# Gated memory of the first mixer: four decay buffers, three broadcast banks, block-wise masks and weights

## The reference

```python
def mlstm_scan(q, k, v, ig, lf, state):
    # h_t = C_t q_t / max(|n_t . q_t|, 1)
    ...
        dmat = jnp.where(tril, bcum[..., :, None] - bcum[..., None, :] + ic[..., None, :], -jnp.inf)
        m_t = jnp.maximum(m_inter, jnp.max(dmat, axis=-1))
        s = jnp.einsum('bhtd,bhsd->bhts', qc, kc) * jnp.exp(dmat - m_t[..., None])
        num = jnp.einsum('bhts,bhse->bhte', s, vc) + w_inter[..., None] * jnp.einsum('bhtd,bhed->bhte', qc, cmat)
        den = jnp.sum(s, axis=-1) + w_inter * jnp.einsum('bhtd,bhd->bht', qc, nvec)
        h = num / jnp.maximum(jnp.abs(den), jnp.exp(-m_t))[..., None]
```

## Time and profile before

| what | us |
|---|---|
| median of 3 runs (2557.1 to 2558.24) | 2557.97 |
| the profiled execution | 2560.64 |
| its span in the profile | 2558.8 |
| TensorE busy in the span | 2370.4 |
| the stage of the change, first row to last `mem_done` (1163.32 to 1234.83) | 71.51 |
| TensorE busy in it | 53.66 |
| VectorE busy in it | 39.92 |
| ScalarE busy in it | 33.42 |

### The profile page before, as it was taken

How to read it: one execution, slowest core, us unless ns; L and a number is a source line. 1 busy time by engine, 2 the same in 40 slices (tenths; PEclk the granted TensorE clock), 3 DMA queues, 4 the chain that set the end, 5 groups by cost and what they waited for, 6 DMA issues and landing times. The chain is left out here.

```text
span 2558.8 us, 36168 instructions
## 1 busy us (share of the span) xinstructions
PE 2370.4 (93%) x13368; PEld 1898.6 (74%) x13368; DVE 1182.8 (46%) x2007; ACT 870.9 (34%) x1369; POOL 160.8 (6%) x140
## 2 busy tenths in 40 slices
PE   4898989999999999987899999999999999987998
PEld 2665778787777777955667777767888877956998
DVE  1423636563443345365553433334343344545665
ACT  1321635552222133245442221224232234235544
POOL 1001120220000010040100000010000010000000
PEclk7998999999999999997999999999999998988999
DMA  7554064236565432300255565552233232303574
GB/s 232 161 165 140 25 174 144 80 108 189 153 213 154 119 99 76 92 16 17 66 154 159 173 189 161 160 164 74 83 110 94 73 108 75 99 1 99 164 207 122
DMA packets 514708, 312.85 MB, mean 122 GB/s; under 512 B 15911, under 2 KB 513166, under 8 KB 514478
## 3 DMA queue, kind: packets, MB, share of 16 engines
q1 hardware_dynamic: 507056, 309.16, 41.2%
q10 hardware_dynamic: 7550, 2.33, 0.4%
HBM read 310.41 MB, written 1.05 MB: 122 GB/s over the span
## 5 line engine op out<-in xcount | busy, mean ns | idle before, releaser
L840 PE MATMUL ps<-h_hi,w_hi 128*128 128x512 f32 (+1 forms) x2208 | 807.1, 366 | 30.9 <-DVE h_lo L1274 13.0
L840 PE MATMUL ps<-h_lo,w_hi 128*128 128x512 f32 (+1 forms) x2208 | 793.4, 359 | 0.0
L840 PE MATMUL ps<-h_hi,w_lo 128*128 128x512 f32 (+1 forms) x2208 | 793.1, 359 | 0.0
L840 PEld LDWEIGHTS ps<-h_hi,w_hi 128*128 128x128 f32 x2208 | 421.5, 191 | 131.5 <-issue 46.3
L1417 DVE TENSOR_TENSOR w_lo<-stage,w_hi 128x1024 fp32r<-128x1024 f32 x244 | 304.8, 1251 | 368.5 <-ACT w_hi L1084 367.9
L840 PEld LDWEIGHTS ps<-h_hi,w_lo 128*128 128x128 f32 x2208 | 421.0, 191 | 68.1
L840 PEld LDWEIGHTS ps<-h_lo,w_hi 128*128 128x128 f32 x2208 | 421.8, 191 | 63.6
L1084 ACT ACTIVATE w_hi<-stage 128x1024 fp32r<-128x1024 f32 x244 | 254.9, 1055 | 476.2 <-PE ps L840 237.9
L1417 DVE TENSOR_TENSOR w_lo<-deep,w_hi 128x1024 fp32r<-128x1024 f32 x184 | 225.2, 1234 | 280.6 <-ACT w_hi L1084 279.2
L840 PE MATMUL ps<-g_hi,w_hi 128*128 128x512 f32 (+1 forms) x704 | 261.0, 371 | 0.3
L840 PE MATMUL ps<-g_lo,w_hi 128*128 128x512 f32 (+1 forms) x704 | 257.6, 366 | 0.0
(11 more groups left out here) (340 smaller groups left out, 2422.7 us busy)
## 6 DMA issues: line engine op xcount, KB each, us to landing
modw<-in_ada_w SPq DMA_DIRECT2D x72, 1024.0 KB
stage<-in_ffn_w_in SPq DMA_DIRECT2D x88, 512.0 KB, 4.6
deep<-in_ffn_w_in SPq DMA_DIRECT2D x88, 512.0 KB, 3.9
modw<-in_w_mod SPq DMA_DIRECT2D x24, 1024.0 KB
stage<-in_w_in SPq DMA_DIRECT2D x44, 512.0 KB, 4.6
stage<-in_ffn_w_out SPq DMA_DIRECT2D x32, 384.0 KB, 3.5
stage<-in_even_w_in SPq DMA_DIRECT2D x24, 512.0 KB, 3.9
deep<-in_ffn_w_out SPq DMA_DIRECT2D x32, 384.0 KB, 3.5
```

What stands on the lines that cost most here:

```text
L840: last = mm(ps[:, j, 0:b - a], w_part[wp][:, u % RING, c, :], x_part[xp][:, x, a:b], start=first and wp == xp, stop=final and wp == "lo")
```

## The change

- Four decay buffers in place of two, of 1280 elements each: two in `big`, one in `vtok`, one in `mixT`. The exponentials of stream j now wait for `numden` of stream j-4.
- Three banks for the broadcast row, 3, 4 and 7, and three `dargs`. `maxima_row(j)` and `args(j)` now wait for `decay` of stream j-3; row 2 waits for the attention's last `att_evac`, which frees bank 7.
- A stream's weights lie by block: `diagonal` (the four blocks of 128x128 in which keys and queries are the same tile), `full` (the one block of tokens and the one of context that is wholly seen) and `across` (context keys for tokens). Only `diagonal` is masked, so `args` is one instruction of 512 elements. The exponentials are eight: four of 128x128 from `dargs`, two of 128x128 and two of 128x256 from the bank.
- `products(h)` is six products of 256 columns in place of two of 512 and two of 256, laid in the banks as the weights are.
- `weighted(j)` is three plain multiplications (512, 256 and 512 elements) in place of four with a factor. The factor 1/8 is left out of numerator and denominator; the floor of the denominator is multiplied by 8 instead.
- Orders: TensorE runs rows 0 to 2 ahead of `products(0)`, and row j+3 in each turn. VectorE runs `weighted(j)`, `memory(j-1)`, `args(j+3)` and then the feed.

```diff
-        decay = big[:, 4 * NT:10 * NT].rearrange("p (s t r q) -> p s t r q", s=2, t=2, r=3)
-        dargs = mixT[:, 0:4, :].rearrange("p (s t) (r q) -> p s t r q", s=2, r=2)
+        decay = [big[:, 4 * NT:4 * NT + 1280], big[:, 7 * NT:7 * NT + 1280], vtok[:, 0:2, :].rearrange("p a d -> p (a d)")[:, 0:1280],
+                 mixT[:, 4:7, :].rearrange("p c n -> p (c n)")[:, 0:1280]]
+        dargs = mixT[:, 0:3, :].rearrange("p s (r a q) -> p s r a q", r=2, a=2)
...
+        ROW_BANK = (3, 4, 7)
@@ TensorE
-                if j >= 2:
-                    eng.wait_ge(S("decay"), p.at("decay", j - 1))
+                if j >= 3:
+                    eng.wait_ge(S("decay"), p.at("decay", j - 2))
+                elif j == 2:
+                    eng.wait_ge(S("att_evac"), p.at("att_evac", N2))
...
                 for a in range(2):
-                    mm(ps[:, a, :], k[:, SEQ + a * P:SEQ + a * P + P], q, start=True, stop=True)
-                    last = mm(ps[:, 2, a * SEQ:a * SEQ + SEQ], k[:, a * P:a * P + P], q[:, 0:SEQ], start=True, stop=True)
+                    near, far = (k[:, at + a * P:at + a * P + P] for at in (0, SEQ))
+                    for bank, keys, at in ((0, near, 0), (1, far, SEQ), (2, far, 0)):
+                        last = mm(ps[:, bank, a * SEQ:a * SEQ + SEQ], keys, q[:, at:at + SEQ], start=True, stop=True)
...
-            maxima_row(0)
+            for j in range(3):
+                maxima_row(j)
             products(0)
-            maxima_row(1)
             for j in range(8):
-                if j + 2 < 8:
-                    maxima_row(j + 2)
+                if j + 3 < 8:
+                    maxima_row(j + 3)
@@ ScalarE
-                if j >= 2:
-                    eng.wait_ge(S("numden"), p.at("numden", j - 1))
-                for a in range(2):
-                    act(decay[:, j % 2, a, 0, :], dargs[:, j % 2, a, 0, :], ACT.Exp, bias=a_of(a))
-                    act(decay[:, j % 2, a, 1, :], ps[:, 3 + j % 2, 0:SEQ], ACT.Exp, bias=a_of(2 + a), scale=-1.0)
-                    last = act(decay[:, j % 2, a, 2, :], dargs[:, j % 2, a, 1, :], ACT.Exp, bias=a_of(2 + a))
+                if j >= 4:
+                    eng.wait_ge(S("numden"), p.at("numden", j - 3))
+                for r in range(2):
+                    for a in range(2):
+                        act(diagonal[:, r, a, :], dargs[:, j % 3, r, a, :], ACT.Exp, bias=a_of(2 * r + a))
+                    act(full[:, r, :], mrow[:, r, 1 - d, :], ACT.Exp, bias=a_of(2 * r + d), scale=-1.0)
+                for s in range(2):
+                    last = act(across[:, s, :], ps[:, ROW_BANK[j % 3], 0:SEQ], ACT.Exp, bias=a_of(2 + s), scale=-1.0)
@@ VectorE
-                if j >= 2:
-                    eng.wait_ge(S("decay"), p.at("decay", j - 1))
...
+                if j >= 3:
+                    eng.wait_ge(S("decay"), p.at("decay", j - 2))
+                up(V.scalar_tensor_tensor(dargs[:, j % 3].rearrange("p r a q -> p (r a) q"), ps[:, ROW_BANK[j % 3], :].rearrange("p (b q) -> p b q", q=P), -1.0,
+                                          mmask[:, j % 2, 0, 0:P].unsqueeze(1).broadcast_to([P, TT, P]), ALU.mult, ALU.add), "args")
...
+                V.tensor_tensor(diagonal, diagonal, qk[:, :, 0::3, :], ALU.mult)
+                V.tensor_tensor(full, full, qk[:, :, 1 + j % 2, :], ALU.mult)
+                up(V.tensor_tensor(across, across, ps[:, 2, :].rearrange("p (s q) -> p s q", s=2), ALU.mult), "weighted")
...
-                link(V.scalar_tensor_tensor(dc, den, -1.0, floor, ALU.mult, ALU.max))
-                link(V.tensor_tensor(dc, den, dc, ALU.max))
+                link(V.scalar_tensor_tensor(dc, floor, HD ** 0.5, den, ALU.mult, ALU.max))
+                link(V.scalar_tensor_tensor(dc, den, -1.0, dc, ALU.mult, ALU.max))
...
             for j in range(8):
                 weighted(j)
+                if j:
+                    memory(j - 1)
+                if j + 3 < 8:
+                    args(j + 3)
                 if j == 2:
                     dve_feed(eng, p, (0, 1))
                 if j == 5:
                     dve_feed(eng, p, (2,))
-                if j + 2 < 8:
-                    args(j + 2)
-                if j:
-                    memory(j - 1)
```

More of the change, by code:

```diff
@@ L1945, in memory @@
                 h, d = j // 2, j % 2
+                diagonal, full, across = decay_parts(j)
                 eng.wait_ge(S("weighted"), p.at("weighted", j + 1))
@@ L1950, in memory @@
                     eng.wait_ge(S("ones_set"), p.at("ones_set", 1))
[L1951 to L1961, removed]
+                for r in range(2):
+                    for a in range(2):
+                        terms = [(diagonal[:, r, a, :], 2 * r + a)]
+                        if a != d:
+                            terms.append((full[:, r, :], 2 * r + d))
+                        if r == 0:
+                            terms += [(across[:, s, a * P:a * P + P], 2 + s) for s in range(2)]
+                        for n, (w, tile) in enumerate(terms):
+                            last = mm(ps[:, 5 + r, a * (P + 1):(a + 1) * (P + 1)], w, vm[:, tile, h, :], start=n == 0, stop=n == len(terms) - 1)
                 up(last, "numden")
-            maxima_row(0)
+            for j in range(3):
+                maxima_row(j)
             products(0)
-            maxima_row(1)
             for j in range(8):
-                if j + 2 < 8:
-                    maxima_row(j + 2)
+                if j + 3 < 8:
+                    maxima_row(j + 3)
                 if j % 2 and j < 7:
@@ L2175, in weighted @@
                 eng.wait_ge(S("qk_done"), p.at("qk_done", j // 2 + 1))
-                for t_ in range(2):
-                    w = decay[:, j % 2, t_]
-                    V.scalar_tensor_tensor(w[:, 1:3, :], ps[:, t_, :].rearrange("p (r q) -> p r q", r=2), HD ** -0.5, w[:, 1:3, :],
-                                           ALU.mult, ALU.mult)
-                    last = V.scalar_tensor_tensor(w[:, 0, :], ps[:, 2, t_ * SEQ:t_ * SEQ + SEQ], HD ** -0.5, w[:, 0, :], ALU.mult, ALU.mult)
-                up(last, "weighted")
+                diagonal, full, across = decay_parts(j)
+                qk = ps[:, 0:2, :].rearrange("p r (b q) -> p r b q", q=P)
+                V.tensor_tensor(diagonal, diagonal, qk[:, :, 0::3, :], ALU.mult)
+                V.tensor_tensor(full, full, qk[:, :, 1 + j % 2, :], ALU.mult)
+                up(V.tensor_tensor(across, across, ps[:, 2, :].rearrange("p (s q) -> p s q", s=2), ALU.mult), "weighted")
             def memory(j):
@@ L2205, in dve_even @@
             eng.wait_ge(S("consts_in"), 16 * (CONST_LOADS + 1))
-            args(0)
-            args(1)
+            for j in range(3):
+                args(j)
             for j in range(8):
                 weighted(j)
+                if j:
+                    memory(j - 1)
+                if j + 3 < 8:
+                    args(j + 3)
                 if j == 2:
```

15 lines of the change are left out of this document (9 added, 6 removed).

## The result

The changed kernel takes 2545.26 us (median of 4 runs, 2539.42 to 2546.94), the kernel before, on the same chip, 2558.1 (4 runs, 2557.1 to 2560.6). The ratio is 0.9944, with a 95% interval of 0.9927 to 0.9962, so it is faster: by 12.8 us between the medians, by 14.3 according to the ratio (9.7 to 18.7 by its interval). The ratio is estimated over all runs of both kernels and need not be the quotient of the medians. The forecast was 2541.7 and a gain of 16.3.

A forecast was written before the change was run, and what follows sets the result against it. TensorE paces the program; its waits and half clock lengthen the 71.5 us stage. A full-clock path of 49.2 plus 3.0 and 3.0 for the clock gives 55.2, gain 16.3: 2557.97 to about 2541.7 us, 8 in 10 within 2535 to 2551.

The forecast's parts named there:

- The start: Stage start on TensorE: rows 1 and 2 fill the gap before products 0, idle 1.6 us in place of 3.05.
- The exponentials: ScalarE, per stream: eight smaller ones taken at 2.45 us, between 1.9 and 3.1; six before took 2.4.
- The products: TensorE: 2.58 us a head at full clock as before, added weight loads at nothing, 2.6 us in all as bound.
- The waits: TensorE ahead of memories: backward 1.9 us each at memories 2, 4 and 6, forward 1.5 at memory 7.
- The feed ahead of `weighted(3)`: VectorE after memory 1: 6.25 us until products 2 may start, against TensorE's 5.2; 1.2 us more with a semaphore.
- The path at full clock: TensorE's stage: memories, products, rows and waits from memory 0 sum to 39.4 us; stage of 49.2 against 71.5.
- The clock: Half clock in the stage: 3.0 us from the fall at the start, 3.0 from one stretch around the feed.
- the step from the profile to the median: Whole program: the gain of 16.3 us taken off the median 2557.97, though the profiled execution lay 2.67 above it.
- the argument that the clock never rose during such work: TensorE's rows and first products: 64-row inputs bring no rise, so the fall at the start should stay.
- full clock throughout: Rival for the stage, chance 0.15: 1.6 us of idleness bring no fall; stage 49.2, gain 22.3, time 2535.7 us.
- The order alone: Rival for the stage, chance 0.15: half-clock busy time stays 34.46 us, costing 17.2; stage 66.4, gain 5.1, time 2552.9.

The follow-up runs named there:

- e1: The changed kernel run and profiled once more, nothing altered: 2542.84 us, ratio 0.9945 to the kernel before, stage 54.61 us.
- e3: The changed kernel with rows 1 and 2 behind the first products on TensorE: 2549.16 us, ratio 0.9963 to the kernel before, stage 58.72 us.
- e8: The kernel before with only row 1 ahead of the first products and VectorE's memory, args, feed order: 2551.94 us, ratio 0.9958, stage 58.27 us.
- e9: The changed kernel with VectorE's two-unit feed one turn later, behind args(6) instead of args(5): 2550.81 us, ratio 0.9963 to the kernel before, stage 58.63 us.
- e5: The changed kernel with six unread filler products of 128 rows ahead of the first products: 2544.92 us, ratio 0.9945 to the kernel before, stage 54.04 us.
- e12: The changed kernel with 128-row fillers wherever TensorE waits and ScalarE's third-unit feed one turn later: 2545.42 us, ratio 0.9942 to the kernel before, stage 51.64 us.
- e2: The changed kernel with two decay buffers in use instead of four: 2544.73 us, ratio 0.9948 to the kernel before, stage 54.79 us.
- e11: The changed kernel with VectorE's args issued once more, unread, for streams 2 to 7: 2546.84 us, ratio 0.9953 to the kernel before, stage 55.88 us.
- e6: The changed kernel with six unread filler products of 64 rows ahead of the first products: 2547.04 us, ratio 0.9940 to the kernel before, stage 55.30 us.
- e7: The kernel before with twelve 128-row fillers each ahead of the first products and memories 2 and 4: 2550.58 us, ratio 0.9958, stage 57.54 us.
- e4: The kernel before with only VectorE's order changed to weighted(j), memory(j-1), args(j+2), then the feed: 2555.49 us, ratio 0.9984, stage 62.26 us.
- e10: The changed kernel with VectorE's feed one turn later and 128-row fillers wherever TensorE waits: 2544.33 us, ratio 0.9938 to the kernel before, stage 54.13 us.

## Why the prediction was right

The size, 16.3 us by the stage, was measured as 16.6; the path with its steps came out nearly term by term. Since the stage of before is the same 71.51 in both, this tests the stage of the changed kernel: 55.2 forecast, 54.93 and 54.61 measured.

- **The start.** Memory 0 was foretold 10.6 us after the first row, at half clock; it came at 11.04 (10.74 in e1). e3 confirms the reason. The idle time ahead of the first products was put at 1.6 us; 3.05 less two rows of 0.86 is 1.33, and 1.33 was measured.
- **The exponentials** were taken at 2.45 us. ScalarE in order of time, stream 0 and the start of stream 1:

```profile
1172.16 0.69 ACT L2078 ACTIVATE big<-mixT,hT 128x128 f32<-128x128 f32 x2
1172.76 0.35 ACT L2079 ACTIVATE big<-ps,hT 128x128 f32<-128x128 f32 x1
1173.01 0.68 ACT L2078 ACTIVATE big<-mixT,hT 128x128 f32<-128x128 f32 x2
1173.60 0.35 ACT L2079 ACTIVATE big<-ps,hT 128x128 f32<-128x128 f32 x1
1173.85 0.83 ACT L2081 ACTIVATE big<-ps,hT 128x256 f32<-128x256 f32 x2
1174.56 0.69 ACT L2078 ACTIVATE big<-mixT,hT 128x128 f32<-128x128 f32 x2
```

  They take 2.40 us, 1172.16 to 1174.56; the six of before took 2.4 too. The Trainium skill ("VectorE: DVE Perf Modes", The TRN2 errata) gives a fixed cost for each instruction, from which 2.39 had been estimated; the trace agrees. Smaller masks saved ScalarE nothing.
- **The products** were taken at 2.58 us a head with their added weight loads at nothing, with 0.64 above that as the bound. With a row beside them and a memory behind, products 1 take 2.79 us (1182.02 to 1184.81); the old ones in e8 take 2.77 in the same place (1183.59 to 1186.36). The added loads thus cost nothing that these rows show. The Trainium skill ("TensorE: Matmul & The Clock Gate", Part 3, The mechanism) has a weight load overlap a matmul only where the row group differs, though it also names a background weight buffer into which a load can be pulled ahead. By the first of these the added loads would show, since the inputs of a head's products all lie in one half of the partitions; they don't, and the measurement decides.
- **The waits.** Backward 1.94 us from a memory's nominal end to the next one's start (1184.81 to 1189.22 less 2.47), foretold 1.9, at memories 2 and 6; with the row inside them, the first two show as 0.86 and 0.80, "about 1" as foretold. At memory 7 the 1.48 is the 1.5 of the sum.
- **The feed ahead of `weighted(3)`** was to delay products 2 by 1.2 us. VectorE there:

```profile
1187.95 1.13 DVE L2212 SCALAR_TENSOR_TENSOR big<-ps,small,big 128x128 f32<-128x128 f32 x4
1188.99 0.68 DVE L2181 SCALAR_TENSOR_TENSOR mixT<-ps,cst 128x512 f32<-128x512 f32 x1
1189.59 2.35 DVE L1417 TENSOR_TENSOR w_lo<-stage,w_hi 128x1024 fp32r<-128x1024 f32 x2
1191.86 0.68 DVE L2189 TENSOR_TENSOR mixT<-mixT,ps 128x512 f32<-128x512 f32 x1
1192.45 0.41 DVE L2190 TENSOR_TENSOR mixT<-mixT,ps 128x256 f32<-128x256 f32 x1
1192.79 0.68 DVE L2191 TENSOR_TENSOR mixT<-mixT,ps 128x512 f32<-128x512 f32 x1
```

  The chain is as written; products 2 waited 0.78. Had I moved the feed for that, e9 shows what would have come.
- **The path at full clock** was summed to 49.2. Read from the rows above with each half-clock piece put at its full-clock length, it is 48.7: 9.8 to memory 0 (9.98 in e5, 9.64 in e12, both at full clock up to there), and then from start to start 2.45 + 2.79 + 4.41 + 4.30 + 2.79 + 4.37 + 2.40 + 2.79 + 4.41 + 3.95 + 4.24 = 38.9 (foretold 39.4). Row 4, costed at 0.86 on the path, lay beside products 1: that pays for products at 2.79 in place of 2.58.
- **The clock** was to cost 3.0 + 3.0 us on that path, in at most two stretches and under 20 us. There are two, 17.1 us. The first costs 3.1 (1.3 at the start, 1.8 in memory 0), the second 3.2 (1.0 in products 2, 2.2 in memory 3 with row 7 behind it). The fall at the start stayed, as foretold; the second lies behind the feed. This is not the luck of one execution: e1, e2 and e11 have the same two stretches.

**What was wrong or weak.** The total fell by 12.8 us between the medians and by 13.7 between the profiled executions, not by 16.3; in e1 it is 17.4 between the medians and 14.1 by the ratio. The stage's end did carry to the end (1323.4 against 1324.0). That the profiled execution reached the stage 3.4 us later is scatter, since in e1 it reached it 2.5 us earlier than the kernel before. What may be more than scatter is the step from the profile to the median: the forecast took the whole 16.3 us, counted from the stage of an execution 2.67 us above the median, off the median itself. If those 2.67 us lie in that stage, it is 68.8 us in a median execution and the gain 13.9, an estimate that would fit the totals; no run shows it.

One reading was wrong. The clock rose at 1219.20 while row 7 and products 3 were running, with their 64-row inputs, 1.4 us after memory 4 had ended:

```profile
1218.75 0.82 PE L1927 MATMUL ps<-big,cst 64*128 64x512 f32 x1
```

So the argument that the clock never rose during such work, which stood against the rival "full clock throughout", had one of the three rises against it. The outcome was right all the same: the fall at the start stayed. What brings it was not known. That it comes after gaps is not enough, as e5 shows, which also goes against that rival, whose condition was the length of the gap alone; and the 64-row inputs are not shown to be the reason, as e5 and e6 fall alike. Here the forecast of the clock leaned on the pattern of before more than on a cause.

The clock's price in the kernel before was put at up to 17.2 us, in one rival; e7 measures 14.0 of 71.5 us, the path above 6.3 in the changed kernel. That makes 7.7 of the 16.6 clock, and the other 8.9 or so schedule, with e7's fillers, and the 3.4 us at half clock left in it, taken as costing nothing. "The order alone", the rival in which the busy time at half clock stays, fell: it went from 34.46 to 16.83. But the kernels e4 and e8 show that the order, in the plain sense, is most of the change: it takes away both the waits and, with them, long stretches at half clock.

## What to carry to other kernels

Sum a path per stage and not per engine, and hold each wait against it: ScalarE's waits for buffers (25.1 us before, 15.0 when they came back in e2) were worth nothing where it was tried, 5 us of waits ahead of two memories, taken away by an order, were worth 9 in the stage and 4 in the total. Before work is taken away, ask what the order alone gives: two moved calls on VectorE and one on TensorE gave 13.2 of 16.6 us of the stage. And before a feed is moved, follow its buffer round to the load that waits for it and the engine that waits for the load.

## What the runs showed of the hardware

- TensorE's granted clock fell to 1.2 GHz behind a stretch in which the engine was busy for 7.16 of 7.96 us (e5), on rows and products with 64-row inputs and six fillers. A long gap is not needed for it: a wait of 0.83 us stood there, and waits of 0.86 to 1.91 in the changed kernel brought none. Nor does the same gap always do the same: the wait of 1.9 us ahead of memory 6 has a fall behind it in e4, e5, e6, e8 and e9, and none in the kernel before, the changed one, e1, e2, e3, e7 and e11. Fillers right there too kept the clock up (e12), but in seven places they still left one fall near products 2, whose wait of 0.78 us is no longer than others without one. In e9 and e10, where products 2 don't wait, no fall came there. What exactly sets the fall stays open.
- A row and products whose inputs lie in different halves of the partitions (the rows' in the lower, those of heads 1 and 3 in the upper) run beside each other: at 1182.02 row 4 and products 1 start together and end by memory 1 at 1184.81, after 2.79 us, what products 3 take alone (1206.27 to 1209.06). In e7 at full clock the row ahead of products 2, which are in the rows' half, took its 0.96 us first (1195.60 to 1196.56).
- Useless matmuls can pay: 36 of them in the kernel before shortened its stage by 14.0 us, and its total by 0.42% (interval 0.26% to 0.58%), 10.8 us.
